# Five edits in a one-core transformer kernel: relu buffers and order of an indexer, order of the experts' transposes, place of a reload

## The chip, the cores and the metric

The kernel runs on one core of a Trainium2 chip. The metric is device time in microseconds (us); the kernel before takes 2500.42 us (median of 3 runs, 2496.2 to 2501.89). The engines are TensorE (PE in the rows; PEld is its weight load), VectorE (DVE), ScalarE (ACT), GpSimd (POOL) and SyncE (SP), which issues most DMAs. Each engine runs its own instruction list in order and waits on semaphores.

## The reference, cut to what matters

A first transformer block (two attentions, then a mixture of experts) is followed by a second block (convolution, a recurrence of RWKV type, a gated feed-forward). All is float32. The parts that the change touches:

```python
# indexer of the sparse attention: 8 heads, query blocks of 128
logits = einsum('bqhd,bkd->bqhk', qii, k_idx) * 64 ** -0.5
score = einsum('bqh,bqhk->bqk', wi, relu(logits))     # then the best 128 keys of each query
# g_a, g_b: 1024 columns each of the first projection, used as sigmoid(g)
# experts: 8 groups of 4 experts
hid = silu(h @ w_gate[e]) * (h @ w_up[e]); out += (hid @ w_down[e]) * combine[:, e]
# second block: h is used again after the recurrence
gates = sigmoid(h @ w_in[:, r_end:] + b_gate)
h = layer_norm(ALPHA * h + y @ w_o)
```

## The kernel before

Activations lie with features on the 128 partitions and tokens along the free axis (512 in the first block, 528 in the second). The program is a row of blocks; at the end of each, all engines meet at a barrier. A float32 product is made of three passes: ACT rounds a weight slab of 128x1024 (`whi`), POOL (in the experts DVE) makes the rest (`wlo`), and TensorE multiplies hi by hi, lo by hi and hi by lo. `pe_tiles` makes such products tile by tile, `tile_loop` is ACT's side of it: weights two tiles ahead, then `take(i)`, which empties the PSUM of tile i.

**Indexer block** (lines 815 to 894). TensorE makes 24 units of logits (three query blocks by 8 heads, 256, 384 and 512 keys wide) into the second half of four PSUM buffers, and 16 tiles of g_a and g_b into the first half. ACT turns a unit's logits into `rel` (relu), of which there are 4 buffers, and DVE adds it, weighted, to `sel`. After the eighth unit of a query block DVE searches the best 128 keys with 16 rounds of `max` and `match_replace`. `logits_after` and `relus_after` say behind which g tile which units come.

**Experts** (lines 1307 to 1605). One loop body per group of experts, 8 bodies. A body uses 24 slabs of 512 KB in the order of `MOE_ORDER`: gate_up of experts 0, 1, 2 (4 slabs each), down 0 (2 slabs), gate_up 3, down 1, 2, 3. They come through a ring of 6 slots: SP loads into a slot once DVE has made the rest of the slab that was in it. `rounds` on ACT and `rests` on DVE work 6 slabs ahead of TensorE and need TensorE to have used the slab 6 before. The inner values of expert e go through `silu(e)` (ACT), `hidden(e)` (DVE), then `turn(e)`: two transposes on TensorE (L1404) into one PSUM bank, ACT copies them rounded (`hid_t_hi`), DVE makes the rest (`hid_t_lo`, L1543); `down(e)` reads both. TensorE's `turn(e)` waits for `hid_made` of e and for `hid_lo` of e-1. The order of these steps is written out by hand on TensorE, ACT and DVE.

**Behind the recurrence.** The buffer of `h` is lent to the recurrence (`kk = h`), and `h` was stored in HBM (`h_spill`, 2112 KB). `group_norm_and_gate` does not use that buffer. `merge` begins with SP loading h back, a wait for it on SP and on ACT, and the load of y; then TensorE makes gate_b from h.

Of the kernel before, what the change touches and what calls it, by code (L numbers as in the profile page):

```python
# [16 lines left out]
ALU = mybir.AluOpType  # L17
ACT = mybir.ActivationFunctionType
AX = mybir.AxisListType.X

P = 128
D = 1024
KD = D // P
# [234 lines left out]
def program(nc, x_t, slabs, moe_slabs, params_d, router_bias, const0, const1, const2, out):  # L258
    top = ExitStack()
    with top:  # L260
# [12 lines left out]
        def sbt(ctx, name, shape, dt=F32):  # L273
            return ctx.enter_context(nc.sbuf_tensor(name, shape, dt))
# [401 lines left out]
        def attention_part(att, xt, h, k1):  # L676
# [33 lines left out]
            with ExitStack() as px:  # L710
# [108 lines left out]
                g_names = ["g_a", "g_b"]  # L819
                g_dests = [ga[:, i, :] for i in range(8)] + [gb[:, i, :] for i in range(8)]  # L820
                with ExitStack() as ix, block() as b:
                    rel = [sbt(ix, f"rel{i}", [P, T1]) for i in range(4)]
                    best = sbt(ix, "best", [P, 8])
                    units = [(qt, hd) for qt in range(1, 4) for hd in range(HEADS)]
                    logits_after = {5: range(16, 20), 6: range(20, 24)}
                    relus_after = {4: range(12, 16), 5: range(16, 20), 11: range(20, 24)}

                    @b.tensor
                    def _(pe):
                        def logits(which):  # L830
                            for u in which:
                                qt, hd = units[u]
                                nk, r0 = (qt + 1) * P, 64 * (hd % 2)
                                if u >= 4:
                                    pe.wait_ge(logit_out, u - 3)
                                nc.tensor.matmul(acc[u % 4][:, 1, 0:nk], qi[r0:r0 + 64, hd // 2, qt * P:(qt + 1) * P],
                                                 ki[r0:r0 + 64, 0:nk], start=True, stop=True).then_inc(logit_ready, 1)

                        logits(range(16))
                        for j, name in enumerate(g_names):  # L840
                            pe_tiles(pe, w, name, KD, 8, hx, T1, g_ready, g_out, first=8 * j,
                                     then=lambda i: logits(logits_after.get(i, ())))

                    @b.scalar
                    def _(act):
                        def relus(which):
                            for u in which:
                                nk = (units[u][0] + 1) * P
                                act.wait_ge(logit_ready, u + 1)
                                if u >= 4:  # L850
                                    act.wait_ge(rel_used, u - 3)
                                nc.scalar.activation(rel[u % 4][:, 0:nk], acc[u % 4][:, 1, 0:nk], ACT.Relu,
                                                     scale=HD ** -0.5).then_inc(logit_out, 1)

                        def take(i):
                            act.wait_ge(g_ready, i + 1)
                            nc.scalar.activation(g_dests[i], acc[i % 4][:, 0, :], ACT.Sigmoid).then_inc(g_out, 1)
                            relus(relus_after.get(i, ()))

                        for n in slab_range("g_a")[:2]:  # L860
                            w.act(act, n)
                        relus(range(12))
                        tile_loop(act, w, [(name, KD, 8) for name in g_names], take)

                    @b.vector
                    def _(dve):
                        for u, (qt, hd) in enumerate(units):
                            nk, s = (qt + 1) * P, sel[qt]
                            dve.wait_ge(logit_out, u + 1)
                            wt = wi[:, qt, hd:hd + 1]  # L870
                            if hd == 0:
                                ins = nc.vector.tensor_scalar(s[:, :], rel[u % 4][:, 0:nk], wt, None, ALU.mult)
                            else:
                                dve.wait_ge(rel_used, u)
                                ins = nc.vector.scalar_tensor_tensor(out=s[:, :], in0=rel[u % 4][:, 0:nk], scalar=wt,
                                                                     in1=s[:, :], op0=ALU.mult, op1=ALU.add)
                            ins.then_inc(rel_used, 1)
                            if hd < HEADS - 1:
                                continue


                            dve.wait_ge(rel_used, u + 1)
                            link("dve", dve, nc.vector.memset(s[0:64, nk - 64:nk], NEG))
                            for _r in range(TOPK // 8):
                                link("dve", dve, nc.vector.max(best[:, :], s[:, :]))
                                link("dve", dve, nc.vector.match_replace(s[:, :], best[:, :], s[:, :], TAKEN))
                            link("dve", dve, nc.vector.tensor_scalar(s[:, :], s[:, :], TAKEN / 2, NEG, ALU.is_gt, ALU.mult))

                    @b.gpsimd
                    def _(pool):  # L890
                        w.all_pool(pool, g_names)

                    @b.sync
                    def _(sp):
                        load_slabs(sp, "g_b")
# [389 lines left out]
        def experts(mx, xt, h, k1):  # L1285
# [21 lines left out]
            with ExitStack() as ex, block() as b:  # L1307
# [56 lines left out]
                def _(pe):  # L1364
# [16 lines left out]
                    def body(n, g):  # L1381
# [43 lines left out]
                        gate_up(1)  # L1425
                        turn(0)
                        gate_up(2)
                        down(0)
                        turn(1)
                        gate_up(3)  # L1430
                        turn_rows(n + 1)
                        turn(2)
                        down(1)
                        turn(3)
                        down(2)
# [7 lines left out]
                def _(act):  # L1443
# [12 lines left out]
                    def body(n, g):  # L1456
# [18 lines left out]
                        turn(0)  # L1475
                        rounds(8, 12)
                        silu(2)
                        rounds(12, 14)
                        turn(1)
                        rounds(14, 18)  # L1480
                        silu(3)
                        slots(n + 1)
                        turn(2)
                        rounds(18, 20)
                        turn(3)
                        rounds(20, 22)
# [16 lines left out]
                def _(dve):  # L1503
# [22 lines left out]
                    def body(n, g):  # L1526
# [26 lines left out]
                        turn(0)  # L1553
                        rests(8, 12)
                        hidden(2)
                        rests(12, 14)
                        turn(1)
                        rests(14, 18)
                        hidden(3)
                        slots(n + 1)  # L1560
                        turn(2)
                        rests(18, 20)
                        turn(3)
                        rests(20, 24)
# [78 lines left out]
        def mixers(rx, h, k2):  # L1643
# [183 lines left out]
            with ExitStack() as wx:  # L1827
                a, wc = sbt(wx, "rw_a", [P, KD, T2]), sbt(wx, "rw_wc", [P, KD, 8])
                kk = h
                decay_and_keys(wa, r, k, v, kk, a, wc, k2)  # L1830

                recurrence(r, k, v, kk, a, a, wc, k2)
                with ExitStack() as gx:
                    group_norm_and_gate(sbt(gx, "gn_scratch", [P, KD, T1]), r, k, v, a, xg, k2)
                merge(h, r, k, a)

        def decay_and_keys(wa, r, k, v, kk, a, wc, k2):
# [613 lines left out]
                    pool.wait_ge(pool_did, len(plan["pool"]))  # L2451


        def group_norm_and_gate(xt, r, k, v, o, xg, k2):

# [4 lines left out]
            with ExitStack() as nx, block() as b:  # L2462
# [112 lines left out]

                @b.sync
                def _(sp):
                    load_slabs(sp, "g_up")

        def merge(h, y, gb, o):  # L2580

# [2 lines left out]
            with ExitStack() as px, block() as b:  # L2584
                hx = Operand(px, "mg", KD, T2)
                w = Weights(px, "mg")
                hx.start(lambda q: h[:, q, :])

                @b.sync
                def _(sp):  # L2590
                    sp.dma_start(h[:, :, :], h_d).then_inc(back, 16)
                    sp.wait_ge(back, 16)
                    sp.dma_start(y[:, :, :], y_d).then_inc(back, 16)
                    load_slabs(sp, "gate_b")
                    sp.wait_ge(back, 32)

                @b.tensor
                def _(pe):
                    pe_tiles(pe, w, "gate_b", KD, 8, hx, T2, g_ready, g_out)

                @b.scalar
                def _(act):
                    act.wait_ge(back, 16)
                    w.begin(act, ["gate_b"], hx)

                    def take(i):
                        act.wait_ge(g_ready, i + 1)
                        nc.scalar.activation(fold(gb[:, i, :], T2), A(i % 4, T2), ACT.Sigmoid,
                                             bias=pcol("b_gate", 8 + i)).then_inc(g_out, 1)

                    tile_loop(act, w, [("gate_b", KD, 8)], take)

                @b.vector
                def _(dve):
                    hx.dve(dve)

                @b.gpsimd
                def _(pool):
                    w.all_pool(pool, ["gate_b"])
# [210 lines left out]
```

## Time and profile before

| | |
|---|---|
| median of 3 runs | 2500.42 us |
| profiled execution | 2511.63 us, its span 2509.9 us |
| granted TensorE clock, mean | 0.904 |
| busy: PE, DVE, ACT, POOL | 85%, 53%, 37%, 30% |
| DMA | 247.92 MB, mean 99 GB/s |
| 198 expert slabs | 512.0 KB each, median 5.2 us from issue to landing |

The span is from the first to the last instruction. A row of the timeline has its start, how long it took, engine, source line, operation, what it writes and reads, and in brackets how long the engine had been idle and what released it. Times are from the span's start.

### The profile page before, as it was taken

What the parts mean: (1) busy time and instruction counts of PE and PEld (TensorE: products, weight loads), DVE (VectorE), ACT (ScalarE), POOL (GpSimd) and SP (SyncE); (2) the same over time, 40 slices, a digit from 0 to 9 for tenths busy, and PEclk for the clock granted to TensorE, in tenths of its full rate; (3) what the DMA queues carried; (4) which work ended last, traced back from release to release, by engine and by line L of the source; (5) the groups of instructions that cost most, each with busy time, mean ns of one, the idle gap of its engine ahead of it and who ended that gap; (6) DMA issues with size and microseconds to landing.
All of it is one profiled execution on the core that took longest, in us unless ns stands there. A gap on an engine that the chain in (4) does not pass through costs nothing. (4 is left out here: it accounts for less than half of the span.)

```text
span 2509.9 us, 45527 instructions
## 1 busy us (share of the span) xinstructions
PE 2123.4 (85%) x19178; PEld 1808.9 (72%) x19178; DVE 1336.6 (53%) x1881; ACT 930.6 (37%) x1463; POOL 749.6 (30%) x375
## 2 busy tenths in 40 slices
PE   4999988788698986699998865888878897999797
PEld 3777735466577775599997834777748897999685
DVE  3354735532778886406997266445432316777502
ACT  3213228621677775522223242222223114333312
POOL 1433300151111211143441345223014414555441
PEclk8998998998799998799999857999679898999899
DMA  3221210021799996132321310000013212232131
GB/s 142 84 76 59 76 51 1 18 84 34 291 325 344 326 347 240 44 93 76 93 93 43 102 43 3 4 4 4 2 57 108 81 43 76 93 93 93 59 94 49
DMA packets 66595, 247.92 MB, mean 99 GB/s; under 512 B 7409, under 2 KB 7409, under 8 KB 65777
## 3 DMA queue, kind: packets, MB, share of 16 engines
q1 hardware_dynamic: 63968, 236.37, 27.8%
q0 software_dynamic: 2448, 8.91, 0.9%
q8 instruction: 143, 2.34, 0.4%
q14 instruction: 36, 0.29, 0.0%
HBM read 232.02 MB, written 13.24 MB: 98 GB/s over the span
## 5 line engine op out<-in xcount | busy, mean ns | idle before, releaser
L1339 DVE TENSOR_TENSOR moe_wlo<-moe_ring,moe_whi 128x1024 fp32r<-128x1024 f32 x198 | 234.7, 1221 | 65.4 <-ACT moe_whi L1335 64.1
L469 PE MATMUL acc<-h_xhi,h_whi 128*128 128x264 f32 x816 | 234.2, 287 | 24.1 <-DVE h_xlo L423 18.3
L469 PE MATMUL acc<-h_xlo,h_whi 128*128 128x264 f32 x816 | 233.3, 286 | 0.0
L469 PE MATMUL acc<-h_xhi,h_wlo 128*128 128x264 f32 x816 | 233.2, 286 | 0.0
L1335 ACT ACTIVATE moe_whi<-moe_ring 128x1024 fp32r<-128x1024 f32 x198 | 204.4, 1059 | 72.7 <-DMA moe_ring<-moe_slabs 45.3
L469 PE MATMUL acc<-ff_xhi,ff_whi 128*128 128x264 f32 x704 | 200.9, 285 | 15.7 <-DVE ff_xlo L423 15.7
L469 PE MATMUL acc<-ff_xlo,ff_whi 128*128 128x264 f32 x704 | 200.3, 284 | 0.0
L469 PE MATMUL acc<-ff_xhi,ff_wlo 128*128 128x264 f32 x704 | 200.1, 284 | 0.0
L378 POOL TENSOR_TENSOR h_wlo<-ring,h_whi 128x1024 fp32r<-128x1024 f32 x51 | 122.5, 2404 | 199.1 <-ACT h_whi L373 199.1
L469 PEld LDWEIGHTS acc<-h_xhi,h_whi 128*128 128x128 f32 x816 | 155.9, 191 | 25.3 <-POOL h_wlo L378 22.6
L1764 DVE SCALAR_TENSOR_TENSOR acc<-cp,par,acc 128x528 f32<-128x528 f32 x232 | 159.2, 766 | 0.0
L378 POOL TENSOR_TENSOR in_wlo<-ring,in_whi 128x1024 fp32r<-128x1024 f32 x39 | 97.7, 2507 | 198.4 <-ACT in_whi L373 198.4
L469 PEld LDWEIGHTS acc<-h_xlo,h_whi 128*128 128x128 f32 x816 | 156.0, 191 | 0.0
L469 PEld LDWEIGHTS acc<-h_xhi,h_wlo 128*128 128x128 f32 x816 | 155.2, 190 | 0.0
L469 PEld LDWEIGHTS acc<-ff_xhi,ff_whi 128*128 128x128 f32 x704 | 133.4, 189 | 16.4 <-POOL ff_wlo L378 15.8
L378 POOL TENSOR_TENSOR ff_wlo<-ring,ff_whi 128x1024 fp32r<-128x1024 f32 x44 | 117.8, 2678 | 91.6 <-ACT ff_whi L373 91.6
L469 PEld LDWEIGHTS acc<-ff_xlo,ff_whi 128*128 128x128 f32 x704 | 133.5, 190 | 0.0
L469 PEld LDWEIGHTS acc<-ff_xhi,ff_wlo 128*128 128x128 f32 x704 | 132.8, 189 | 0.0
L469 PE MATMUL acc<-in_xhi,in_whi 128*128 128x512 f32 (+1 forms) x280 | 118.8, 424 | 15.6 <-DVE in_xlo L423 15.6
L469 PE MATMUL acc<-in_xhi,in_wlo 128*128 128x512 f32 (+1 forms) x280 | 110.9, 396 | 0.0
L469 PE MATMUL acc<-in_xlo,in_whi 128*128 128x512 f32 (+1 forms) x280 | 110.7, 395 | 0.0
L2746 DVE SCALAR_TENSOR_TENSOR ff_t<-ff_up,par,ff_t 128x528 f32<-128x528 f32 x44 | 108.4, 2465 | 1.6
(477 smaller groups left out, 5586.6 us busy)
## 6 DMA issues: line engine op xcount, KB each, us to landing
ring<-slabs SPq DMA_DIRECT2D x213, 512.0 KB, 3.5
moe_ring<-moe_slabs SPq DMA_DIRECT2D x198, 512.0 KB, 5.2
tok_rows<-h_tok SPq DMA_DIRECT2D x5, 512.0 KB, 3.0
h_spill<-x SPq DMA_DIRECT2D x1, 2112.0 KB, 9.8
y_spill<-cp SPq DMA_DIRECT2D x1, 2112.0 KB, 7.4
x<-h_spill SPq DMA_DIRECT2D x1, 2112.0 KB, 10.0
rw_r<-y_spill SPq DMA_DIRECT2D x1, 2112.0 KB, 8.2
xt<-x_t SPq DMA_DIRECT2D x1, 2048.0 KB, 7.4
```

Of the source, the lines that this page charges most:

```text
L378: nc.gpsimd.tensor_tensor(self.lo[n % self.depth][:, :], ring[n % RING][:, :], self.hi[n % self.depth][:, :].bitcast(F32), ALU.subtract).t ...
L469: mm = nc.tensor.matmul(acc[j][0:rows, s, 0:t1 - t0], wp[:, at:at + rows], xp[:, t0:t1], start=(k == 0 and m == 0), stop=(k == kt - 1 and ...
L1335: nc.scalar.activation(whi[u % AHEAD][:, :], ringm[u % AHEAD][:, :], ACT.Copy).then_inc(w_hi, 1)
L1339: tensor_tensor(wlo[u % AHEAD][:, :], ringm[u % AHEAD][:, :], whi[u % AHEAD][:, :].bitcast(F32), ALU.subtract).then_inc(w_lo[u % 2], 1)
L1764: ins = nc.vector.scalar_tensor_tensor(out=d, in0=x, scalar=tap(q, j), in1=csum(q), op0=ALU.mult, op1=ALU.add)
L2746: nc.vector.scalar_tensor_tensor(out=d, in0=up[i % 4][:, 2:2 + T2], scalar=tap(2), in1=d, op0=ALU.mult, op1=ALU.add).then_inc(tapped, 1)
```

## The change

1. Indexer: four more relu buffers, which lie in `gb[:, 4..7]` (the results of g tiles 12 to 15 are stored there later, so `take(12)` now waits for all 24 units). ACT makes 16 units ahead of the g tiles where it made 12, TensorE 20 units of logits where it made 16. The last eight relus follow g tiles 3 and 4 where the last twelve followed 4, 5 and 11; the last four logits follow tile 4 where the last eight followed 5 and 6.
2. Experts: on TensorE, ACT and DVE `turn(1)` and `turn(2)` each come one place earlier.
3. The reload of h is issued in `group_norm_and_gate`; `merge` neither issues it nor waits for it.

No line of the diff changes how many columns any stage computes.

```diff
-  rel = [sbt(ix, f"rel{i}", [P, T1]) for i in range(4)]
-  logits_after = {5: range(16, 20), 6: range(20, 24)}
-  relus_after = {4: range(12, 16), 5: range(16, 20), 11: range(20, 24)}
+  rel = [sbt(ix, f"rel{i}", [P, T1]) for i in range(4)] + [gb[:, 4 + i, :] for i in range(4)]
+  logits_after = {4: range(20, 24)}
+  relus_after = {3: range(16, 20), 4: range(20, 24)}
 # TensorE
-  logits(range(16))
+  logits(range(20))
 # ScalarE
-      if u >= 4:
-          act.wait_ge(rel_used, u - 3)
-      nc.scalar.activation(rel[u % 4][:, 0:nk], acc[u % 4][:, 1, 0:nk], ACT.Relu,
+      if u >= 8:
+          act.wait_ge(rel_used, u - 7)
+      nc.scalar.activation(rel[u % 8][:, 0:nk], acc[u % 4][:, 1, 0:nk], ACT.Relu,
 ...
   act.wait_ge(g_ready, i + 1)
+  if i == 12:
+      act.wait_ge(rel_used, 24)
 ...
-  relus(range(12))
+  relus(range(16))
 # experts, TensorE
   gate_up(2)
+  turn(1)
   down(0)
-  turn(1)
+  turn(2)
   gate_up(3)
   turn_rows(n + 1)
-  turn(2)
   down(1)
 # experts, ScalarE (VectorE alike, with rests and hidden)
   silu(2)
+  turn(1)
   rounds(12, 14)
-  turn(1)
+  turn(2)
   rounds(14, 18)
   silu(3)
   slots(n + 1)
-  turn(2)
   rounds(18, 20)
 # group_norm_and_gate, SyncE
+  h_back = sem("gn_h_back")
+  sp.dma_start(h[:, :, :], h_d).then_inc(h_back, 16)
   load_slabs(sp, "g_up")
+  sp.wait_ge(h_back, 16)
 # merge, SyncE
-  sp.dma_start(h[:, :, :], h_d).then_inc(back, 16)
-  sp.wait_ge(back, 16)
   sp.dma_start(y[:, :, :], y_d).then_inc(back, 16)
   load_slabs(sp, "gate_b")
-  sp.wait_ge(back, 32)
+  sp.wait_ge(back, 16)
 # merge, ScalarE
-  act.wait_ge(back, 16)
   w.begin(act, ["gate_b"], hx)
```

ACT's list in the indexer block before, from the first relus (L852; L373 rounds a weight slab, L857 is `take`):

```order
L852 ACTIVATE rel<-acc 128x256 x8
L852 ACTIVATE rel<-acc 128x384 x4
...
L857 ACTIVATE h<-acc 128x512
L852 ACTIVATE rel<-acc 128x384 x4
L373 ACTIVATE in_whi<-ring 128x1024
L857 ACTIVATE h<-acc 128x512
L852 ACTIVATE rel<-acc 128x512 x4
```

And now (relu is L853, `take` is L860):

```order
L853 ACTIVATE rel<-acc 128x256 x4
L853 ACTIVATE gb<-acc 128x256 x4
L853 ACTIVATE rel<-acc 128x384 x4
L853 ACTIVATE gb<-acc 128x384 x4
...
L860 ACTIVATE h<-acc 128x512
L853 ACTIVATE rel<-acc 128x512 x4
L373 ACTIVATE in_whi<-ring 128x1024
L860 ACTIVATE h<-acc 128x512
L853 ACTIVATE gb<-acc 128x512 x4
```

The second query block (384 keys) is now whole ahead of the g tiles, and the third (512 keys) follows tiles 3 and 4 in place of 5 and 11.

VectorE's list in the body of the experts before (L1537 is `hidden`, L1339 a slab's rest, L1543 `hid_t_lo`, L1524 the rests of the next group's tokens), from `hidden(2)` on:

```order
L1537 SCALAR_TENSOR_TENSOR hid<-silu,comb_slots,acc 128x256
...
L1339 TENSOR_TENSOR moe_wlo<-moe_ring,moe_whi 128x1024
L1543 TENSOR_TENSOR hid_t_lo<-acc,hid_t_hi 128x256
...
L1537 SCALAR_TENSOR_TENSOR hid<-silu,comb_slots,acc 128x256
...
L1524 TENSOR_TENSOR h_slots_lo<-acc,h_slots_hi 128x512
L1543 TENSOR_TENSOR hid_t_lo<-acc,hid_t_hi 128x256
```

And now (each line number is 3 higher):

```order
L1540 SCALAR_TENSOR_TENSOR hid<-silu,comb_slots,acc 128x256
L1546 TENSOR_TENSOR hid_t_lo<-acc,hid_t_hi 128x256
...
L1342 TENSOR_TENSOR moe_wlo<-moe_ring,moe_whi 128x1024
L1546 TENSOR_TENSOR hid_t_lo<-acc,hid_t_hi 128x256
...
L1540 SCALAR_TENSOR_TENSOR hid<-silu,comb_slots,acc 128x256
...
L1527 TENSOR_TENSOR h_slots_lo<-acc,h_slots_hi 128x512
```

`hid_t_lo` of expert 1 now stands right behind `hidden(2)`, and that of expert 2 ahead of `hidden(3)` and the tokens' rests, not behind them.

SP's list behind the recurrence before (L333 loads weight slabs):

```order
L333 DMA ring<-slabs 128x1024 x2
L2462 UNCONDITIONAL_BRANCH
L2589 UNCONDITIONAL_BRANCH
L2591 DMA x<-h_spill 128x4224
L2593 DMA rw_r<-y_spill 128x4224
L333 DMA ring<-slabs 128x1024 x8
```

And now:

```order
L2582 DMA x<-h_spill 128x4224
L333 DMA ring<-slabs 128x1024 x2
L2465 UNCONDITIONAL_BRANCH
L2595 UNCONDITIONAL_BRANCH
L2597 DMA rw_r<-y_spill 128x4224
L333 DMA ring<-slabs 128x1024 x8
```

The load of h stands one block earlier, ahead of two slab loads that wait for the last products of the group-norm block.

## Rows read from the trace of the kernel before

**Rows 1.** Timeline of VectorE, indexer block: the waits for relus and its end.
```profile
245.75 4.95 DVE L875 SCALAR_TENSOR_TENSOR sel<-rel,wi,sel 128x384 f32<-128x384 f32 x4 [10.53 <-ACT rel L852]
...
288.22 5.40 DVE L875 SCALAR_TENSOR_TENSOR sel<-rel,wi,sel 128x512 f32<-128x512 f32 x4 [11.88 <-ACT rel L852]
...
318.12 0.43 DVE L887 TENSOR_SCALAR sel<-sel 128x512 f32<-128x512 f32 x1
```
**Rows 2.** Timeline of ScalarE, indexer block: `take` of tiles 7, 8 and 15.
```profile
265.34 0.60 ACT L857 ACTIVATE h<-acc 128x512 f32<-128x512 f32 x1 [6.04 <-PE acc L469]
...
270.78 0.60 ACT L857 ACTIVATE gb<-acc 128x512 f32<-128x512 f32 x1 [3.89 <-PE acc L469]
...
308.86 0.60 ACT L857 ACTIVATE gb<-acc 128x512 f32<-128x512 f32 x1 [4.84 <-PE acc L469]
```
**Rows 3.** Timeline of TensorE, start of the block behind the indexer.
```profile
319.15 6.77 PE L469 MATMUL acc<-cc,ring 128*96 128x512 f32 x12 [10.33 <-PEq L821]
...
326.63 2.74 PE L469 MATMUL acc<-cc,ring 128*96 128x512 f32 x6
```
**Rows 4.** Timeline behind the recurrence: DVE, SP, ACT, PE in turn.
```profile
1869.03 0.71 DVE L2546 TENSOR_TENSOR rw_a<-rw_a,acc 128x528 f32<-128x528 f32 x1 [1.07 <-PE acc L2476]
1870.23 0.33 SPq L2591 DMA_DIRECT2D x<-h_spill  x1
...
1880.20 1.06 ACT L373 ACTIVATE mg_whi<-ring 128x1024 fp32r<-128x1024 f32 x1 [13.44 <-DMA x<-h_spill]
...
1884.42 0.56 PE L469 MATMUL acc<-mg_xhi,mg_whi 128*128 128x264 f32 x1 [15.50 <-DVE mg_xlo L423]
```
**Rows 5.** Waits of SyncE's DMA queue over the whole program: total us, times, longest.
```profile
SPq L333 <- PE acc L2476: 63.8, 1, 63.8
```
**Rows 6.** Waits, experts stage (655 to 985): total us, times, longest.
```profile
ACT moe_whi L1335 <- DMA moe_ring<-moe_slabs: 33.2, 54, 2.4
...
PE acc L1404 <- DVE hid_t_lo L1543: 25.7, 8, 3.7
```
**Rows 7.** Timeline of TensorE, third group: `turn(1)`, `turn(3)`, matmuls of `down(2)`.
```profile
759.12 0.38 PE L1404 MATMUL acc<-c,hid 128*128 128x128 f32 x2
...
772.56 0.66 PE L1404 MATMUL acc<-c,hid 128*128 128x128 f32 x2 [3.67 <-DVE hid_t_lo L1543]
...
773.44 0.63 PE L1417 MATMUL acc<-moe_whi,hid_t_lo 128*128 128x512 f32 x1
773.87 0.63 PE L1417 MATMUL acc<-moe_wlo,hid_t_hi 128*128 128x512 f32 x1
...
776.23 0.39 PE L1417 MATMUL acc<-moe_wlo,hid_t_hi 128*128 128x512 f32 x1
776.46 0.39 PE L1417 MATMUL acc<-moe_whi,hid_t_hi 128*128 128x512 f32 x1
```
**Rows 8.** Timeline of VectorE, third group: `hidden(2)` and `hidden(3)`.
```profile
761.45 0.48 DVE L1537 SCALAR_TENSOR_TENSOR hid<-silu,comb_slots,acc 128x256 f32<-128x256 f32 x1
...
770.41 0.48 DVE L1537 SCALAR_TENSOR_TENSOR hid<-silu,comb_slots,acc 128x256 f32<-128x256 f32 x1
```
**Rows 9.** Timeline, other groups: fifth `turn(3)`, then seventh `turn(1)`, `hidden(2)`, `turn(3)`.
```profile
853.51 0.41 PE L1404 MATMUL acc<-c,hid 128*128 128x128 f32 x2 [2.46 <-DVE hid_t_lo L1543]
...
921.89 0.38 PE L1404 MATMUL acc<-c,hid 128*128 128x128 f32 x2
...
923.12 0.47 DVE L1537 SCALAR_TENSOR_TENSOR hid<-silu,comb_slots,acc 128x256 f32<-128x256 f32 x1
...
934.83 0.41 PE L1404 MATMUL acc<-c,hid 128*128 128x128 f32 x2 [3.18 <-DVE hid_t_lo L1543]
```
**Rows 10.** Stretches: length, busy PE PEld DVE ACT POOL, clock, DMA share, GB/s.
```profile
823.00:863.00 40.00, 37.54 (x170) 30.61 (x169) 33.30 (x40) 31.29 (x40) 7.65 (x4) 0.96 0.94 345
...
904.00:943.00 39.00, 35.82 (x169) 29.29 (x168) 33.08 (x41) 31.23 (x40) 6.59 (x4) 1.00 0.95 344
...
762.00:764.00 2.00, 2.00 (x11) 1.65 (x10) 1.06 (x2) 1.10 (x2) 0.00 (x0) 1.00 1.02 418
```

More of the change, by code:

```diff
@@ L871, in _ @@
                             if hd == 0:
-                                ins = nc.vector.tensor_scalar(s[:, :], rel[u % 4][:, 0:nk], wt, None, ALU.mult)
+                                ins = nc.vector.tensor_scalar(s[:, :], rel[u % 8][:, 0:nk], wt, None, ALU.mult)
                             else:
                                 dve.wait_ge(rel_used, u)
-                                ins = nc.vector.scalar_tensor_tensor(out=s[:, :], in0=rel[u % 4][:, 0:nk], scalar=wt,
+                                ins = nc.vector.scalar_tensor_tensor(out=s[:, :], in0=rel[u % 8][:, 0:nk], scalar=wt,
                                                                      in1=s[:, :], op0=ALU.mult, op1=ALU.add)
@@ L1555, in body @@
                         hidden(2)
+                        turn(1)
                         rests(12, 14)
-                        turn(1)
+                        turn(2)
                         rests(14, 18)
@@ L1560, in body @@
                         slots(n + 1)
-                        turn(2)
                         rests(18, 20)
@@ L1833, in mixers @@
                 with ExitStack() as gx:
-                    group_norm_and_gate(sbt(gx, "gn_scratch", [P, KD, T1]), r, k, v, a, xg, k2)
+                    group_norm_and_gate(sbt(gx, "gn_scratch", [P, KD, T1]), r, k, v, a, xg, k2, h)
                 merge(h, r, k, a)
@@ L2451, in _, with group_norm_and_gate @@
                     pool.wait_ge(pool_did, len(plan["pool"]))
-        def group_norm_and_gate(xt, r, k, v, o, xg, k2):
+        def group_norm_and_gate(xt, r, k, v, o, xg, k2, h):
             meaned, centred, squared, varred, rooted = (sem("gn_" + n) for n in ("meaned", "centred", "squared", "varred", "rooted"))
```

## The prediction

> **What bounds the kernel now.** I read first the page's busy line and its slices, then the idle gaps of TensorE in the timeline, and for each gap at an edited place who released it. TensorE is busy 85% of the span and no other engine more than 53%, so what counts is what TensorE waits for, and what it does at the lower of its two clocks (1.2 in place of 2.4 GHz) after a wait. The change touches three such places.
>
> First, the indexer block. TensorE's last tile there is taken by ACT at 308.86 to 309.46 [rows 2], but the next block starts at 319.15, after 10.33 us of idle [rows 3]. What ends last is VectorE at 318.55, and VectorE itself had twice waited for relus, 10.53 and 11.88 us [rows 1], not because they could not be made but because ACT's list had them behind g tiles 4 and 11.
>
> Second, the experts. TensorE waits eight times, once in each group, for `hid_t_lo` at `turn(3)`: 25.7 us in all [rows 6]. That value stands on VectorE behind `hidden(3)` and the tokens' rests. But DMA is close: ACT's slab steps wait 33.2 us for slabs [rows 6], and the DMA share over a group is 0.94 to 0.95 [rows 10].
>
> Third, behind the recurrence. Work ends at 1869.74, SP issues the load of h at 1870.23, and ACT starts at 1880.20, released by that load; TensorE starts at 1884.42 [rows 4].
>
> **Part 1, indexer.** VectorE's two waits go. The relus of units 12 to 15 are made ahead of the g tiles, before VectorE ends its first search, and those of 16 to 23 behind tiles 3 and 4, long before VectorE asks. Without them its work ends at 318.55 - 10.53 - 11.88 = 296.1, so VectorE is no longer last. TensorE and ACT are. Tiles follow each other every 270.78 - 265.34 = 5.44 us; ahead of a tile with four logits in front of it ACT is idle 6.04 us, ahead of the next 3.89 [rows 2]. Two such insertions become one, which saves 2.15. The other four logits go ahead of tile 0, where TensorE follows the relus anyway and those follow VectorE's first eight units. The sixteenth relu is released at the moment at which the twelfth was, by VectorE's eighth unit, so I charge 0.1. The last `take` ends at 309.46 - 2.15 + 0.1 = 307.4. From the last engine's end to TensorE's next matmul it takes 319.15 - 318.55 = 0.6, so the next block starts at 308.0 in place of 319.15: 11.1 us. The wait added in `take(12)` costs nothing: its 24 units are done one search before VectorE's end, a search being 318.55 - 293.62 = 24.9 long [rows 1], so at 271, and that take comes three tiles before the last, at about 290; were it late, all of ACT's weight slabs for tiles 14 and 15 would stand behind it. There is one more piece. The first 12 matmuls of the next block take 6.77 us at the low clock it starts with, while 6 take 2.74 once it is up, so 12 about 5.3 [rows 3]. A gap of 1.2 us in place of 10.33 should leave the clock up: 1.4 more. Part 1 is 12.5. Bounds: 9.0 (309.46 + 0.6 = 310.1 if the insertion saves nothing and the clock falls all the same) to 13.
>
> **Part 2, experts.** Expert 2's rest no longer stands behind expert 3's steps, so `turn(3)` does not wait for it. But TensorE now has `turn(2)` ahead of gate_up(3), and that needs `hidden(2)`. In the third group `turn(1)` stood at 759.12, behind `down(0)` [rows 7]. The new list brings TensorE to `turn(2)` 0.2 later, at 759.3. `hidden(2)` starts at 761.45 [rows 8]; behind it VectorE makes expert 1's rest, 0.4 us each, so `turn(2)` starts at 761.45 + 0.9 = 762.35, a new wait of 3.0. This is the worst of the eight groups. In the seventh the same steps are 921.89 and 923.12 [rows 9], a wait of 1.9, and the distances of the eight groups from `turn(1)` to `hidden(2)` add up to 11.6 us, so the new waits are 11.6 + 8 x 0.7 = 17.2 us in all. From `turn(2)`, gate_up(3), the tokens' transposes and `down(1)` take 9.4 (from 759.12 to 768.89, where TensorE's wait of 3.67 begins, less two short transposes), so TensorE reaches `turn(3)` at 771.75. `hidden(3)` began at 770.41 [rows 8], and what stands ahead of it on ACT and VectorE is as much as before (`turn(2)` in the slot that `turn(1)` left), so it is done by 770.9. `turn(3)` is thus 0.8 earlier than 772.56. In the seventh group it would be at 933.4 in place of 934.83, 1.4 earlier. Over all eight groups, worked the same way, the gain is 9.7 us.
>
> Then the clock. After the wait in the third group the matmuls of `down(2)` start 0.43 apart, later 0.23 [rows 7]; eight of them are slow, 1.6 us. A fall follows seven of the eight waits, even the one of 2.46; only the seventh group, with 3.18, has none [rows 9], runs at 1.00 and is 39 us long instead of 40 to 41 [rows 10]. So length alone does not decide, and a wait of about 2.2 will still bring a fall in some groups. I take four in place of seven: 3 x 1.6 = 4.8. Part 2 is 9.7 + 4.8 = 14.5. Bounds: 0, if slabs arrive no sooner, to 21 (no fall at all, 9.7 + 7 x 1.6). `turn(1)` ahead of `down(0)` is free: its two transposes are there in either list, and expert 0's rest is made during gate_up(2).
>
> Here the Trainium skill speaks for more. Its page "TensorE: Matmul & The Clock Gate", section "HAM oscillation — how this bites in real kernels", says that a long enough wait in every round of a loop restarts every round at the low clock and that short ones do not. By that rule the trace's seven falls are explained, and by it alone, taking every new wait but the third group's as short, the part would be near 20.
>
> **Part 3, h.** The load is issued at the start of the group-norm block, where SP otherwise waited 63.8 us [rows 5] for that block's last products, and needs 10. Nothing there reads or writes that buffer. The two slab loads behind it in the list wait for those products anyway. ACT then starts when the barrier opens, at 1870.3 in place of 1880.20: 9.9 us, and TensorE at 1874.5. Left is y's load, now issued at once, beside the two slab loads of 1 MB; ACT wants the first of these 6 us after its start. At 2.1 + 1.0 MB and the 345 GB/s of the experts' stretch [rows 10] all is in by 9 us, the slabs issued first. Clock: TensorE begins the block low in both kernels. Bounds 7 to 11.
>
> **Sum.** 12.5 + 14.5 + 9.9 = 36.9. The profiled execution, 2511.63 us with a span of 2509.9, becomes 2474.7 (span 2473.0). The runs are 11 us faster than the profiled one, a distance I keep: 2500.4 - 36.9 = 2463.5.
>
> **Rivals.**
> - Slabs are the bound of the experts. For it: share 0.94 to 0.95, and ACT's waits for slabs just before `silu(3)`. Against: the seventh group, 39 us, shows that a group without a fall keeps what it gains, and 418 GB/s in one stretch of that stage [rows 10] where the group's mean is 345. If they give the whole of part 2 back: 2500.4 - 22.4 = 2478.0. A chance of 0.18.
> - The new waits are too short for any fall; then 4 x 1.6 = 6.4 more: 2457.1. For it: they are 1.9 to 2.2 but for one. Against: the fall after 2.46. A chance of 0.17.
> - One of the two sure terms is short: y's load holds up gate_b's slabs (part 3 gives 5), or `take(12)` or the slabs behind relus hold TensorE in the indexer (part 1 gives 8): 2468. A chance of 0.07.
> - Slower: the experts get both waits. If `hidden(3)` moved back with the later gate_up(3), `turn(3)` would still wait its 3.2 and the new 2.2 with a fall of 1.6 would come on top, 8 x 3.8 = 30 us, against 22.4 from the rest: 2508. It decides from 2.8 us lost in each group. For it: gate_up(3) ends about 2 us later, and ACT's four slab steps ahead of `silu(3)` need its slabs used. Against: those steps were at 764 to 768 because slabs came then, and the slabs are used by 768.1. A chance of 0.03.
> - The change in its words speaks of 516 columns; no line of the diff makes fewer of them, so nothing is counted for it.
>
> On the DMA rival the Trainium skill is on its side. "DMA: Bandwidth & Descriptors", section "Where 436 GB/s comes from", says that for HBM to SBUF the HBM side binds at about 358 GB/s for a core. By it a group's 13.6 MB take 38.0 us, and the gain could not exceed 8 x 2.8 = 22. The 418 GB/s above speak against it as a hard limit.
>
> **How the numbers follow.** The computed case has 0.55 and its own range is 2457 to 2470. The range of 8 in 10 takes in the first two rivals in most of their width: from 2453 (all upper bounds but one) to 2480 (part 2 nothing and part 1 at its lower bound). A measurement of this kernel tells about 0.2%, 5 us, from no change. Every case but the slower one is faster by more than that: faster 0.96, same 0.01, slower 0.03.
>
> **What would show it.** Right: the block behind the indexer starts near 308 and VectorE's list in it ends near 296; gate_b's first ACT step right behind the barrier and no wait for h; at `turn(3)` no wait above 0.5 us, and at `turn(2)` one of about 2 us in each group; groups of about 39 us. Wrong: ACT's waits for slabs grown by as much as TensorE's went, a gap at `turn(3)` that stays above 2 us, or a stage outside these three that changes by more than 3 us.

## The result and the profile after

The changed kernel takes 2473.91 us in the median of 4 runs (2458.85 to 2477.77), the kernel before 2500.95 in 4 runs beside it: a ratio of 0.9881, 95% interval 0.9843 to 0.9918. The prediction was 2463.5, in a range of 2453 to 2480. The gain is 27.0 us where 36.9 were forecast; with all later runs pooled it is 32.1 (means 2502.3 of 48 runs of before, 2470.2 of 11 of the changed kernel). The profiled execution of the changed kernel took 2458.85 (span 2457.1), the lowest of all its runs; that of before, 2511.63, was the highest of its own. The two traces therefore differ by 52.8 us, 21 more than the kernels do. The three edits, read in these traces one by one, give 12.7, 17.3 and 9.9.

The head of the page of the changed kernel (busy us, share of the span, instructions; then the granted clock in 40 slices):

```profile
PE 2099.0 (85%) x19178; PEld 1789.1 (73%) x19178; DVE 1341.1 (55%) x1881; ACT 930.5 (38%) x1463; POOL 750.6 (31%) x375
...
PEclk8998998998899998899999858999789899999899
```

**Indexer.** TensorE's first logits, in the kernel before and in the changed one (start, busy, what; idle before it in brackets):

```profile
206.06 2.08 PE L836 MATMUL acc<-ki,qi 64*128 64x256 f32 x8 [1.05 <-PEq L718]
```
```profile
203.54 2.08 PE L837 MATMUL acc<-ki,qi 64*128 64x256 f32 x8 [1.05 <-PEq L718]
```

Timeline of the changed kernel, ScalarE's last `take` and then TensorE's next block:

```profile
304.43 0.60 ACT L860 ACTIVATE gb<-acc 128x512 f32<-128x512 f32 x1 [4.84 <-PE acc L469]
```
```profile
305.39 5.36 PE L469 MATMUL acc<-cc,ring 128*96 128x512 f32 x12 [1.00 <-PEq L821]
...
311.45 2.74 PE L469 MATMUL acc<-cc,ring 128*96 128x512 f32 x6
```

The gap of 10.33 us [rows 3] is 1.00, and the first 12 matmuls take 5.36 in place of 6.77. The next block starts 13.76 us earlier, but 2.52 of these were there at the first logits already, before anything that the edit touches. From the first logits to the next block it is 113.09 us before and 101.85 now: 11.24 less, and with the 12 matmuls 12.7. All nine profiles with this part, of this kernel and of those below, have 101.8 to 101.9 us there, and the four with the old lists and four buffers 113.1 to 113.5. (The recorded expectations below work with 11.7. It comes from an offset of 3.5 us, taken at 163.5 us, of which 1.0 is lost again before the first logits, where both kernels have the same code.) Of VectorE's two waits [rows 1] none is left, and its last step there ends at 293.1.

```profile
292.69 0.43 DVE L890 TENSOR_SCALAR sel<-sel 128x512 f32<-128x512 f32 x1
```

**Experts.** Waits in the stage (640 to 950 us; total us, times, longest), to be held against [rows 6]:

```profile
ACT moe_whi L1338 <- DMA moe_ring<-moe_slabs: 25.0, 49, 2.1
...
PE acc L1407 <- DVE hid_t_lo L1546: 13.7, 8, 1.9
...
PE acc L1420 <- DVE hid_t_lo L1546: 1.9, 5, 0.5
```

ACT waits less for slabs than before, 25.0 us in place of 33.2. All eight waits on L1407 are now at `turn(2)`. The third group, in time order of each engine (ACT: a round, `silu(2)`, `turn(1)`; VectorE: four rests, `hidden(2)`, `turn(1)`; TensorE: `turn(1)`, `turn(2)`, `turn(3)`):

```profile
737.04 1.06 ACT L1338 ACTIVATE moe_whi<-moe_ring 128x1024 fp32r<-128x1024 f32 x1 [0.22 <-DMA moe_ring<-moe_slabs]
738.00 0.37 ACT L1468 ACTIVATE silu<-acc 128x256 f32<-128x256 f32 x1
738.27 0.38 ACT L1447 ACTIVATE hid_t_hi<-acc 128x256 fp32r<-128x256 f32 x1
```
```profile
734.90 4.62 DVE L1342 TENSOR_TENSOR moe_wlo<-moe_ring,moe_whi 128x1024 fp32r<-128x1024 f32 x4
739.44 0.47 DVE L1540 SCALAR_TENSOR_TENSOR hid<-silu,comb_slots,acc 128x256 f32<-128x256 f32 x1
739.84 0.41 DVE L1546 TENSOR_TENSOR hid_t_lo<-acc,hid_t_hi 128x256 fp32r<-128x256 f32 x1
```
```profile
735.37 0.38 PE L1407 MATMUL acc<-c,hid 128*128 128x128 f32 x2
...
740.39 0.41 PE L1407 MATMUL acc<-c,hid 128*128 128x128 f32 x2 [1.84 <-DVE hid_t_lo L1546]
...
749.81 0.38 PE L1407 MATMUL acc<-c,hid 128*128 128x128 f32 x2
```

`silu(2)` ends at 738.37, but VectorE gets to `hidden(2)` only at 739.44, behind four rests of 1.15 us each. `turn(3)`, which waited 3.67 in that group [rows 7], doesn't wait. Two stretches of a group each, one without a fall of the clock and one with (us; busy PE, PEld, DVE, ACT, POOL; clock, DMA share, GB/s):

```profile
721.00:759.00 38.00, 35.89 (x168) 29.09 (x167) 32.84 (x41) 30.87 (x40) 6.82 (x3) 1.00 0.97 356
873.00:912.00 39.00, 37.15 (x167) 29.97 (x166) 33.20 (x40) 30.75 (x40) 6.97 (x3) 0.96 0.93 336
```

The stage (first matmul of the first group to the last of the eighth) went from 326.3 to 309.0 us.

**Behind the recurrence**, in place of [rows 4]: SP's issue of y's load, ACT's first step of gate_b, TensorE's first matmul.

```profile
1826.33 0.33 SPq L2597 DMA_DIRECT2D rw_r<-y_spill  x1
1826.35 1.06 ACT L373 ACTIVATE mg_whi<-ring 128x1024 fp32r<-128x1024 f32 x1 [3.52 <-PEq L2465]
...
1830.55 0.56 PE L469 MATMUL acc<-mg_xhi,mg_whi 128*128 128x264 f32 x1 [5.57 <-DVE mg_xlo L423]
```

The 13.44 us that ACT was idle, ended by h's load, are 3.52 ended by the barrier; TensorE's gap fell from 15.50 to 5.57.

### The profile page after: what moved, and what is told of

It is laid out like the page before. It is cut to its first block and busy times, and to the rows that moved or that the text cites. A ratio compares the mean times of both kernels' runs of the same rounds, so it can differ in the third digit from the quotient of the medians.

```text
span 2457.1 us, 45524 instructions
## 1 busy us (share of the span) xinstructions
PE 2099.0 (85%) x19178; PEld 1789.1 (73%) x19178; DVE 1341.1 (55%) x1881; ACT 930.5 (38%) x1463; POOL 750.6 (31%) x375
```

## The experiments

All are held against runs of before on the same chip. The first four tell the parts apart.

**p1_indexer, p2_experts, p3_h: one part each; after_again: all three.** The edits are the pieces of the diff above: the indexer's lists and buffers; the order of `turn` in the experts' three lists; the load of h in the group-norm block.

> Only the indexer's part of the change (eight logit buffers, the twenty units ahead of the g tiles). Theory (three independent terms, each worth what the two traces show at its place): the block behind the indexer starts 11 to 12 us earlier, and the timed run is 11.7 us faster than before (ratio 0.9953). Rival (the first gap only moves the point at which TensorE's clock falls, and later stages give part of it back): under 8 us faster, with the start of the next block still 11 us earlier.

> Only the experts' part of the change (the turns of experts 1 and 2 moved ahead). Theory: eight waits of 3.2 us at the fourth expert's turn become eight of about 1.8 at the third's, and most of the clock falls after them go: 17 us faster (ratio 0.993), the stage 326 to 309 us long. Rival 1 (the profiled execution of the changed kernel was a lucky one, and in most executions the clock still falls after several of the new waits): 10 to 12 us, the profile with three falls or more. Rival 2 (the slabs bound the stage): under 8 us, and ACT's waits for slabs up by 10 us or more.

> Only the reload of h a block earlier. Theory: 9.9 us between the end of the group-norm block and ACT's first step of gate_b, and 9.9 us in the time (ratio 0.996). Rival: gate_b's slabs or the clock behind the shorter gap take back 3 us or more, so 5 to 7.

> All three parts, the changed kernel once more, timed beside its parts. Theory (the terms add): the sum of the three parts alone, 36 to 39 us faster. Rival (the clock takes back what the parts give one by one, since the median so far moved by only 27): 25 to 30 us, less than the sum of the three by 8 or more, with a lower mean clock than the 0.919 of the first profiled execution and at least three clock falls behind the experts' waits.

Measured:

| kernel | median us (runs) | before (runs) | ratio, 95% |
|---|---|---|---|
| p1_indexer | 2487.28 (6) | 2501.97 (19) | 0.9936 (0.9918 to 0.9954) |
| p2_experts | 2491.13 (8) | 2501.97 | 0.9951 (0.9933 to 0.9969) |
| p3_h | 2496.81 (12) | 2501.97 | 0.9980 (0.9968 to 0.9991) |
| after_again | 2471.06 (6) | 2501.97 | 0.9877 (0.9856 to 0.9898) |

The parts give 14.7, 10.8 and 5.2 us, 30.7 together, and all at once 30.9: they add. The rival of after_again, a sum that falls short of its parts, is out, though two of its signs came (a mean clock of 0.917 and three clock falls in the profile); the theory's 36 to 39 is out too. The experts are worth what the first rival of p2_experts said. Their stage is 312.0 us with two clock falls, where that rival wanted three, and these rows of p2_experts (655 to 975 us) answer to [rows 6]:

```profile
ACT moe_whi L1335 <- DMA moe_ring<-moe_slabs: 24.3, 42, 2.1
PE acc L1404 <- DVE hid_t_lo L1543: 14.1, 8, 2.5
```

So the new waits are as in the changed kernel. Chance was less in its trace, a fast one, than in that of before, a slow one. p3_h has the old order of the experts, and yet its profiled execution shows

```profile
PE acc L1404 <- DVE hid_t_lo L1543: 21.3, 8, 3.5
```

21.3 us of waits in place of 25.7, five falls in place of seven, and a stage of 318.7. Its gap behind the recurrence is that of the changed kernel, to the hundredth:

```profile
1864.38 0.56 PE L469 MATMUL acc<-mg_xhi,mg_whi 128*128 128x264 f32 x1 [5.57 <-DVE mg_xlo L423]
```

Yet the timed gain is half of the 9.93 us by which the gap is shorter; p3_h's profiled execution (2491.42) was again the fastest of its 12.

**s10 and s11: `silu(2)` and `hidden(2)` ahead of two, or one, of the slab steps.** In the changed kernel the wait at `turn(2)` hangs on VectorE's list. For s10 (s11 has 11 for 10):

```diff
-                        rounds(8, 12)
+                        rounds(8, 10)
                         silu(2)
                         turn(1)
-                        rounds(12, 14)
+                        rounds(10, 14)
...
-                        rests(8, 12)
+                        rests(8, 10)
                         hidden(2)
                         turn(1)
-                        rests(12, 14)
+                        rests(10, 14)
```

> The changed kernel with silu(2), hidden(2) and turn(1) moved ahead of the last two of rounds(8, 12) and rests(8, 12). Theory (TensorE's new wait at the third expert's turn hangs only on the place of hidden(2) in VectorE's list, behind the rest of a slab that TensorE needs much later): the eight waits of 1.8 us at that turn go (13.7 us to under 2), groups of 36.6 us in place of 38.3, 13 us faster than the changed kernel, 2458 as a median. Rival (the slabs take over: they already have a share of 0.97 of the group at 356 GB/s): the wait moves to the slabs, groups of about 38, ACT's waits for slabs up by 10 us or more, 0 to 4 us faster than the changed kernel.

> The same with only one round and one rest moved behind silu(2) and hidden(2). Theory (place in VectorE's list): one rest is 1.15 us, so each of the eight waits goes from 1.8 to about 0.7, 9 us faster than the changed kernel. Rival (slabs): 0 to 4 us faster, as with two moved.

s10: 2467.65 (6 runs) against 2506.70 (11), ratio 0.9868 (0.9841 to 0.9894). s11: 2469.39, ratio 0.9856 (0.9828 to 0.9885). The changed kernel had 0.9877 (0.9856 to 0.9898) on another chip, so neither is shown to be faster. Timeline of s10's TensorE, `turn(2)` and `turn(3)` of one group:

```profile
747.30 0.38 PE L1407 MATMUL acc<-c,hid 128*128 128x128 f32 x2
...
758.08 0.44 PE L1407 MATMUL acc<-c,hid 128*128 128x128 f32 x2 [1.27 <-DVE hid L1540]
```

The wait at `turn(2)` is gone, as the theory has it, and another has come at `turn(3)`, for `hidden(3)`. What holds that back is in ACT's list between the two: four rounds, each idle for its slab, then `silu(3)`.

```profile
751.46 1.06 ACT L1338 ACTIVATE moe_whi<-moe_ring 128x1024 fp32r<-128x1024 f32 x1 [0.59 <-DMA moe_ring<-moe_slabs]
752.74 1.06 ACT L1338 ACTIVATE moe_whi<-moe_ring 128x1024 fp32r<-128x1024 f32 x1 [0.21 <-DMA moe_ring<-moe_slabs]
754.02 1.06 ACT L1338 ACTIVATE moe_whi<-moe_ring 128x1024 fp32r<-128x1024 f32 x1 [0.22 <-DMA moe_ring<-moe_slabs]
755.31 1.06 ACT L1338 ACTIVATE moe_whi<-moe_ring 128x1024 fp32r<-128x1024 f32 x1 [0.23 <-DMA moe_ring<-moe_slabs]
756.28 0.36 ACT L1468 ACTIVATE silu<-acc 128x256 f32<-128x256 f32 x1
```

The rival (0 to 4 us) was right on the result: the stage is 308.7 us in s10 and 306.1 in s11, against 309.0 and 311.8 in the two profiles of the changed kernel. Its sign, ACT's waits for slabs up by 10 us, did not come: they were 22.1 us in s10 between 650 and 945 us, and 25.0 in the changed kernel. The number that tells is the period of a group, not the wait.

**s10_half and after_half: half of each slab's bytes**, with s10's order and with the changed kernel's. The second half of each slab is not loaded, so both kernels leave out part of the experts' weights.

```diff
-                        sp.dma_start(ringm[u % AHEAD][:, :], moe_slabs[bass.ds(g * PER + u, 1)]
+                        sp.dma_start(ringm[u % AHEAD][:, 0:512], moe_slabs[bass.ds(g * PER + u, 1), :, 0:512]
```

> The kernel with two steps moved, and in the experts' loop each slab load brings only the first 512 of 1024 columns (the other half is left as it was, so the experts compute with wrong weights). It halves the bytes of the slabs and leaves every step of ACT, VectorE and TensorE. Theory (slabs don't bind): within 3 us of the kernel with full slabs. Rival (slabs bind once the wait at the turn is gone): groups of 36.5 us, 10 us or more faster than with full slabs.

> The changed kernel with the same halved slab loads (experts compute with wrong weights). Theory (in the changed kernel TensorE's wait at the third expert's turn hangs on VectorE's list, not on slabs): the waits stay at 1.5 us or more and the time within 4 us. Rival (slabs hold up the rests ahead of hidden(2)): the waits fall below 0.8 us each and the time by 8 us or more.

s10 with full slabs and with half, one group each:

```profile
721.00:759.00 38.00, 36.08 (x169) 29.26 (x168) 33.09 (x41) 30.76 (x40) 6.98 (x3) 1.00 0.97 361
```
```profile
727.00:764.00 37.00, 36.35 (x171) 29.54 (x170) 32.99 (x41) 30.97 (x40) 7.27 (x4) 1.00 0.63 198
```

With half the bytes s10's stage falls from 308.7 to 296.2 us, TensorE's waits for `hidden(3)` at `turn(3)` go from 11.0 us to 0.3, and TensorE is busy 36.35 of 37.00 us. So slabs bound s10. In after_half the eight waits at `turn(2)` stay:

```profile
PE acc L1407 <- DVE hid_t_lo L1546: 13.0, 8, 1.9
```

Its stage is 304.9 us, against 309.0 in the first profile of the changed kernel: in that kernel the waits hang on VectorE's list and not on slabs. With half the bytes its groups take 38.0 us each, and with full slabs those without a fall 38.0 to 38.5. The limit that the slabs set is thus close to the one that VectorE's list sets, and either cure alone gives little in the stage. By time the theory of after_half missed: it had said within 4 us, its rival 8 or more, and the mean of its two runs is 12.5 us below that of the 11 of the changed kernel, give or take 7 with so few runs. The profile shows 4.1 us in the stage and 6.2 over the span; the rest stays open. The timed medians, 2457.93 and 2457.73 in 2 runs each, can't tell the two halved kernels apart; the profile of s10_half was 8.4 us later before the experts began, 7 of them by a clock stretch that is told below.

**without_h, without_indexer, without_experts: the changed kernel less one part.** A second measure of each term.

> The changed kernel without its third part (h is loaded where it was). Theory (the early load is worth its 9.9 us less what TensorE's clock takes back behind the shorter gap, some 3 to 4): 6 to 7 us slower than the changed kernel, 26 us faster than before. Rival (the full 9.9 counts, and the small gain of this part alone was scatter): 9.9 us slower than the changed kernel, 22 to 23 faster than before.

> The changed kernel without its first part. Theory (what the traces show at the indexer, 11.7 us, is what it is worth, and the 15 of this part alone were in part scatter): 11.7 us slower than the changed kernel, 20 to 21 faster than before. Rival (without the gap of 10.3 us the clock in the stages behind keeps a better phase): 15 or more slower than the changed kernel, and the clock's low stretches from 360 to 600 us of the span longer than with it.

> The changed kernel without its second part. Theory (the experts' stage is 324 us in the mean with the old order and 311 with the new; the two profiled executions first compared were one long and one short): 12 to 13 us slower than the changed kernel, with a stage of 319 to 327 us in the profile. Rival (the part is worth the 17.3 us read first): 17 us slower than the changed kernel, 15 faster than before.

2473.90, 2481.06 and 2481.56 us (6 runs each), ratios to before 0.9901 (0.9879 to 0.9922), 0.9917 (0.9899 to 0.9935) and 0.9919 (0.9900 to 0.9939). A least-squares fit with one term for each part to the 91 runs (36 of before beside these kernels, then those of the parts, of the pairs and of the whole; s10, s11 and the halves left out) gives, with 95% intervals: indexer 13.7 ± 2.2 us, experts 12.4 ± 2.1, h 6.4 ± 2.0, together 32.5. h comes out as the theory of without_h had it. For the indexer both the theory's 11.7 and the 12.7 read above are inside, and the rival's sign is not there: the low stretches between 360 and 600 us are no longer without the part. For the experts the stage without the part is 319.3 us, and the 17.3 of the first two traces lie outside.

**rel8_old_order: eight logit buffers, old order.** The kernel before with `rel` of eight (and the wait in `take(12)` that these need), but logits and relus in fours behind tiles 4, 5 and 11.

```diff
-                    rel = [sbt(ix, f"rel{i}", [P, T1]) for i in range(4)]
+                    rel = [sbt(ix, f"rel{i}", [P, T1]) for i in range(4)] + [gb[:, 4 + i, :] for i in range(4)]
...
-                                if u >= 4:
-                                    act.wait_ge(rel_used, u - 3)
+                                if u >= 8:
+                                    act.wait_ge(rel_used, u - 7)
```

> The kernel before with eight logit buffers but with the logits and relus in their old places (groups of four behind tiles 4, 5 and 11). Theory (the order in ACT's list makes VectorE wait, and the buffers only allow another order): VectorE still waits about 10.5 and 11.9 us, the next block starts at 319 us, and the time is that of before. Rival (four buffers were what held the relus back): both waits shorter, the next block earlier by 5 us or more, 5 to 12 us faster than before.

2500.62 us (10 runs) against 2500.22 (17), ratio 0.9995 (0.9978 to 1.0013): no gain that the time shows. VectorE:

```profile
243.60 4.94 DVE L877 SCALAR_TENSOR_TENSOR sel<-gb,wi,sel 128x384 f32<-128x384 f32 x4 [5.09 <-ACT gb L852]
...
286.07 5.40 DVE L877 SCALAR_TENSOR_TENSOR sel<-gb,wi,sel 128x512 f32<-128x512 f32 x4 [11.88 <-ACT gb L852]
```

The second wait is what it was. The first is 5.4 us shorter, which the theory did not foresee, but only 2.4 of these are gained: counted from the first logits (206.27 here, 206.06 before) it ends 2.4 us earlier, and VectorE comes to it 3.1 us later. The eight buffers let the g tiles begin that much earlier, and from the first logits to the next block it is 110.7 us in place of 113.1. Half of that is given back at once: the first 12 matmuls of the next block take 7.98 us in place of 6.77. TensorE's gap stays 10.33 us, as VectorE is still last. Of the 11.2 us that the block gains in the changed kernel 8.9 need the new order. The new order with four buffers was not run.

## Why the prediction was right, and where it was too large

The mechanisms were all there, in the places named; the sum was 36.9 and the runs fit 32.5. Parts 1 and 2 together were forecast at 27.0 and fit 26.1, so nearly all of the difference is part 3.

**Part 1, indexer: 12.5 forecast, 12.7 in the first trace, 13.7 ± 2.2 timed.** With the 2.5 us by which this execution was early at the first logits, VectorE's end is at 293.1 + 2.5 = 295.6, forecast 296.1; the last `take` ends at 305.0 + 2.5 = 307.5, forecast 307.4; the next block starts at 305.4 + 2.5 = 307.9, forecast 308.0. The first 12 matmuls take 5.36 us, forecast 5.3. Each piece of the sum is there.

**Part 2, experts: 14.5 forecast, 12.4 ± 2.1 timed.** The new wait at `turn(2)` is there in each group, and its cause, `hidden(2)`, is the one named. It was forecast at 17.2 us in all and measures 13.7; falls were forecast at four and were one and three in the two profiles of the changed kernel. That would make the part larger than forecast. The forecast lies at the upper edge of what was timed. Two things that the working had not pull the other way:

1. The eight waits and seven falls of [rows 6] are one execution. The stage with the old order took 326.3 us there and in p1_indexer, 325.7 in rel8_old_order, but 318.7 in p3_h and 319.3 in without_experts (mean 323.3). With the new order it took 309.0, 311.8, 312.0 (p2_experts), 308.9 (without_indexer) and 308.3 (without_h), mean 310.0. The difference of the means is 13.3, so some 3 us of the forecast were in the trace that it was read from.
2. What fewer falls and shorter waits give back in a group is kept only down to the slabs' period. A group without a fall took 38.0 to 38.5 us in the changed kernel, and the eight of s11, with no fall and shorter waits at the turns, 306.1 / 8 = 38.3. In the changed kernel itself this costs little, some 0.2 us a group against the 38.0 of after_half; it is the next step that it takes whole. The rival on slabs was thus wrong for this step and right for the next one: the 418 GB/s of 2 us [rows 10], held against it in the prediction, do not last, and whole groups without a fall moved 354 to 365 in the changed kernel, s10 and s11. The Trainium skill's page "DMA: Bandwidth & Descriptors", section "Where 436 GB/s comes from", has the HBM side bind at about 358 GB/s for a core; over whole groups the traces agree within 2% (354 to 365). No run shows whether it is that limit which holds them there, or the ring of six slots; that fewer bytes shorten s10's groups fits both.

The page "TensorE: Matmul & The Clock Gate" of the Trainium skill (section "HAM oscillation — how this bites in real kernels") lets the clock fall after long waits in a loop and not after short ones. The traces bear out its direction. In five profiles with the old order the clock fell after 31 of 40 waits (most 2.5 to 3.7 us long). In the six with the new order, after_half among them, it fell after 8 of 48 (all but the first of each profile 1.8 to 2.5 us). In most cases the short wait goes without a fall and the long one with it, but not in all: 1.85 had a fall, 3.18 [rows 9] had none. But the gain of near 20 that the prediction worked out by that rule did not come: that working counted all seven falls of one trace as gained but one, and in the mean over the traces there were 6.2 before and 1.6 after, without the halved kernel.

**Part 3, h: 9.9 forecast, 6.4 ± 2.0 timed.** The step in the trace is exact: 15.50 to 5.57 us. The term is what was mis-sized: it put what follows behind the gap at nothing. From gate_b's first matmul to the end of the span all profiles run the same code. Five have the late load: there it takes 621.9, 622.0, 622.1 and 623.5 us, and 625.4 in the profile of before. Nine have the early load: 625.2 to 625.3 in four, 626.3 to 626.5 in five. The means are 623.0 and 625.9, so 2.9 us come back; the gap is 9.6 us shorter in the mean, and 6.7 are left, close to the 6.4 that was timed. One piece is a wait in the last projection (waits of p3_h behind 1990 us):

```profile
PE acc L469 <- POOL fd_wlo L378: 2.3, 1, 2.3
```

All nine with the early load have it, and of the five others only that of before, so the first two traces could not show the loss. Low stretches of the clock go with it: some 188 us behind gate_b's first matmul it is low for 17.1 us in these ten and for 13.7 in the other four. Why the early load brings this, when the code there is the same, stays open. The runs' mean clocks say the same: with two levels, 1.2 and 2.4 GHz, a run's time at the lower is 2 x span x (1 - mean clock). In p3_h the low stretch at the gap is 6.8 us where before has 17.1, but the mean over its 12 runs is 460, against 462 in the 19 runs of before beside them, so some 8 us more lie elsewhere. In both profiles of the changed kernel the clock stayed low to 12 us behind the gap, and gate_b took 53.4 and 53.2 us to its next long gap, but in p3_h 50.6, so this is not bound to the edit:

```profile
1830.50:1845.00 14.50, 12.99 (x64) 12.40 (x65) 8.60 (x7) 6.00 (x8) 5.13 (x2) 0.58 0.57 218
```
```profile
1864.40:1878.90 14.50, 12.63 (x87) 12.11 (x88) 8.54 (x7) 5.93 (x8) 7.51 (x3) 0.86 0.60 226
```

The first is the changed kernel, the second p3_h, each from the restart: 64 matmuls in 14.5 us at a clock of 0.58, 87 at 0.86.

**The base.** The prediction kept the distance of 11 us between the profiled execution and the median. That was sound for the time, but the experts' term was read from a trace that was slow at the very place edited, and h's from one that had the later loss already. The later loss was in no term, and the width of the range took it in: the range of the computed case alone, 2457 to 2470, was missed by the first median, and the pooled mean of 2470.2 lies at its edge. The wide range's lower end is not the sum of its own bounds: 13 + 21 + 11 from 2500.4 is 2455.4, not 2453. The signs of "wrong" that it named came partly: two stages outside the edits changed by 3 us or more, the first one (3.5) and the group norm (5.1, clock 0.72 to 0.85 in its second half). p3_h has its group norm as before, so both are differences between executions and not the change.

## What to carry to other kernels

When a wait is cut out of a loop that also streams weights, work out the transfers' own period first: here the first reorder brought a group without a clock fall to 38.0 to 38.5 us, above TensorE's own 37.0 (s10_half) but already at the slabs' 38.3 (s11), so the second did not pay. Size a term from several executions where the clock falls in some and not in others; two traces can be 20 us off between them. When a gap is shortened, compare the stages behind it too, over several profiles: here 2.9 of 9.6 us were lost there. To find a part's worth in a trace, count from the last instruction ahead of it and not from an earlier mark. More buffers alone gave nothing that the time showed: most of the gain needed the order of the lists that uses them.

## What the runs showed of the hardware

The scatter of this kernel (2494 to 2512 us) goes with the clock. Over 48 runs of before the time rises by 0.33 us for each us at the low level, with a correlation of 0.84.

One place has several outcomes. Some 63 us behind a gap of 2.28 us the clock falls, at 420 to 426 us (433 to 438 where the indexer is the old one), and stays low for 6.8 us or for 23.9, in three profiles for 17.1 or 20.5, in kernels whose code there is the same. The changed kernel, then without_h (same code up to the recurrence), stretches 414 to 440 and 440 to 470:

```profile
414.00:440.00 26.00, 19.92 (x133) 10.38 (x130) 13.96 (x72) 21.95 (x88) 0.00 (x0) 0.87 0.00 1
440.00:470.00 30.00, 22.47 (x191) 13.30 (x189) 14.81 (x53) 22.89 (x71) 0.00 (x0) 1.00 0.00 1
```
```profile
414.00:440.00 26.00, 21.86 (x138) 11.99 (x136) 12.74 (x69) 20.65 (x84) 0.00 (x0) 0.72 0.00 1
440.00:470.00 30.00, 23.91 (x160) 13.22 (x160) 15.95 (x60) 22.67 (x73) 0.00 (x0) 0.85 0.00 1
```

From that gap to the one of 9.9 us near 600 it is 230 us with the short stretch (before, p3_h, without_indexer, changed kernel twice, after_half) and 237 with the long (p1_indexer, s10, s11, s10_half, without_h); the other three have 234 to 237 (without_experts, p2_experts, rel8_old_order). These 7 us are more than half of what each part of this change is worth, and the granted clock is what tells of them.
